# Row norms of a two-block transformer: squares as the moving operand on four column strips instead of as the stationary one

## The reference, cut to what matters

```python
def _rms_norm(x, g):
    xf = x.astype(jnp.float32)
    y = xf * lax.rsqrt(jnp.mean(xf * xf, axis=-1, keepdims=True) + EPS)
    return (y * g.astype(jnp.float32)).astype(x.dtype)
...
        h = _modulate(x, g_pre_mix[l], sx1, cx1)
        x = x + gx1 * _rms_norm(_token_mixer(h, kv_ctx, rope, lp, lam, lam_init), g_post_mix[l])
        hm = _modulate(x, g_pre_mlp[l], sx2, cx2)
        x = x + gx2 * _rms_norm(_sq_relu_mlp(hm, w_ff1[l], w_ff2[l]), g_post_mlp[l])
```

## Time and profile before

| | us |
|---|---|
| median of three runs | 3958.98 |
| lowest and highest run | 3958.79, 3963.68 |
| span of the profiled execution | 3959.9 |
| TensorE busy | 3646.2 (92%) |
| VectorE busy | 1911.9 (48%) |
| ScalarE busy | 1398.4 (35%) |
| GpSimd busy | 131.7 (3%) |

### The profile page before, as it was taken

How to read it: one execution, slowest core, us unless ns; L and a number is a source line. 1 busy time by engine, 2 the same in 40 slices (tenths; PEclk the granted TensorE clock), 3 DMA queues, 4 the chain that set the end, 5 groups by cost and what they waited for, 6 DMA issues and landing times. The chain is left out here.

```text
span 3959.9 us, 47862 instructions
## 1 busy us (share of the span) xinstructions
PE 3646.2 (92%) x18756; PEld 2836.1 (72%) x18756; DVE 1911.9 (48%) x2912; ACT 1398.4 (35%) x2388; POOL 131.7 (3%) x90
## 2 busy tenths in 40 slices
PE   6989898979999999998897999989998999989999
PEld 2878897855677778884773567778887776677767
DVE  0756565655544354441475654434443346433553
ACT  2454433224443322222423444332222435334342
POOL 0000000010000010001001000010001000000000
PEclk9999898999999989997998999989998999989999
DMA  8425453320112323326331112223332221222212
GB/s 312 149 91 155 123 165 129 100 70 28 47 60 69 107 64 93 94 91 266 123 92 36 43 49 64 85 71 95 96 96 87 67 65 51 70 89 66 60 45 94
DMA packets 97407, 371.75 MB, mean 94 GB/s; under 512 B 11184, under 2 KB 11440, under 8 KB 95280
## 3 DMA queue, kind: packets, MB, share of 16 engines
q1 hardware_dynamic: 97200, 368.82, 29.2%
HBM read 357.25 MB, written 11.53 MB: 93 GB/s over the span
## 5 line engine op out<-in xcount | busy, mean ns | idle before, releaser
L368 DVE TENSOR_TENSOR w_lo<-w_raw,w_hi 128x1024 fp32r<-128x1024 f32 x527 | 644.9, 1224 | 776.7 <-ACT w_hi L358 776.4
L382 PE MATMUL banks<-h_hi,w_hi 128*128 128x512 f32 (+2 forms) x2040 | 790.3, 387 | 28.2 <-DVE h_lo L1005 9.8
L384 PE MATMUL banks<-h_hi,w_lo 128*128 128x512 f32 (+2 forms) x2040 | 749.5, 367 | 0.0
L383 PE MATMUL banks<-h_lo,w_hi 128*128 128x512 f32 (+2 forms) x2040 | 749.3, 367 | 0.0
L358 ACT ACTIVATE w_hi<-w_raw 128x1024 fp32r<-128x1024 f32 x545 | 573.0, 1053 | 363.6 <-DMA w_raw<-in_stream 361.6
L382 PEld LDWEIGHTS banks<-h_hi,w_hi 128*128 128x128 f32 (+1 forms) x2040 | 391.1, 192 | 118.6 <-issue 35.5
L384 PEld LDWEIGHTS banks<-h_hi,w_lo 128*128 128x128 f32 (+1 forms) x2040 | 390.1, 191 | 66.4
L383 PEld LDWEIGHTS banks<-h_lo,w_hi 128*128 128x128 f32 (+1 forms) x2040 | 391.9, 192 | 56.6 <-issue 3.8
L382 PE MATMUL banks<-merged_hi,w_hi 128*128 128x512 f32 (+1 forms) x960 | 350.0, 365 | 28.1 <-PEq L2320 10.7
L384 PE MATMUL banks<-merged_hi,w_lo 128*128 128x512 f32 (+1 forms) x960 | 346.4, 361 | 0.0
L383 PE MATMUL banks<-merged_lo,w_hi 128*128 128x512 f32 (+1 forms) x960 | 345.6, 360 | 0.0
(11 more groups left out here) (322 smaller groups left out, 4988.6 us busy)
## 6 DMA issues: line engine op xcount, KB each, us to landing
w_raw<-in_stream SPq DMA_DIRECT2D x593, 512.0 KB, 3.6
w_whole<-in_stream SPq DMA_DIRECT2D x48, 512.0 KB, 8.9
x_kept<-x SPq DMA_DIRECT2D x4, 2048.0 KB, 7.2
x<-x_kept SPq DMA_DIRECT2D x4, 2048.0 KB, 8.1
dft_table<-in_dft SPq DMA_DIRECT2D x2, 2048.0 KB, 8.1
x<-in_x SPq DMA_DIRECT2D x1, 2048.0 KB, 11.2
out_x<-x SPq DMA_DIRECT2D x8, 256.0 KB, 4.4
late_consts<-in_consts SPq DMA_DIRECT2D x1, 1152.0 KB, 5.5
```

The source lines that it names most:

```text
L368: (by or self.nc.vector).tensor_tensor(self.lo[:, c], self.raw[:, c], self.hi[:, c].bitcast(F32), ALU.subtract)\
L382: self.nc.tensor.matmul(out, w_hi, x_hi, start=start, stop=False)
L383: self.nc.tensor.matmul(out, w_hi, x_lo, start=False, stop=False)
L384: mm = self.nc.tensor.matmul(out, w_lo, x_hi, start=False, stop=stop)
```

## The change

The sum of a norm over features is made the other way round. sum does nothing until four tiles are squared, and then issues four matmuls, one for each tile: the stationary operand is a 128x32 block of ones, the moving operand the whole tile of squares (512 or 256 columns), and matmul j writes 32 PSUM partitions from 32 j. The second four accumulate onto the first. A new step gather (VectorE) copies the 128 x NT result to sq[:, 0], and a new step fold (TensorE) adds the four lanes by NT/128 matmuls with the copy as the stationary operand and one column of the constant fold as the moving one; it leaves the totals with tokens on the partitions, where root reads them. average is gone. square of tile 4 to 7 now waits for the first group of four, where it waited for one tile. A bank is used for the lanes (7, or 6 where the norm's neighbour uses 7). The root of following and of the second hybrid layer's norm is taken in the stage that computes the sums.

```diff
     def square(self, act, k, src):
-        if k >= 4:
-            act.wait_ge(self.summed.sem, self.summed.at(k - 3))
+        if k >= self.LANES:
+            act.wait_ge(self.summed.sem, self.summed.at(k // self.LANES))
...
     def sum(self, pe, k):
+        if k % self.LANES < self.LANES - 1:
+            return
         pe.wait_ge(self.squared.sem, self.squared.at(k + 1))
+        for j in range(self.LANES):
+            rows = slice(self.LANE * j, self.LANE * (j + 1))
+            mm = self.K.nc.tensor.matmul(self.lane_sums[rows], self.K.const("ones")[:, 0:self.LANE], self.sq[:, j],
+                                         start=k < self.LANES, stop=k == self.n - 1, tile_position=(0, self.LANE * j))
+        mm.then_inc(self.summed.sem, 1)
+
+    def gather(self, dve):
+        dve.wait_ge(self.summed.sem, self.summed.at(self.groups))
+        self.K.nc.vector.tensor_copy(self.sq[:, 0], self.lane_sums).then_inc(self.gathered.sem, 1)
+
+    def fold(self, pe):
+        pe.wait_ge(self.gathered.sem, self.gathered.at(1))
         for i in range(self.nt):
-            at = k * self.nt + i
-            mm = self.K.nc.tensor.matmul(self.sums[:, at:at + 1], self.sq[:, k % 4, i * P:(i + 1) * P],
-                                         self.K.const("ones")[:, 0:1], start=True, stop=True)
-        mm.then_inc(self.summed.sem, 1)
-
-    def average(self, dve):
-        dve.wait_ge(self.summed.sem, self.summed.at(self.n))
-        self.K.nc.vector.reduce_sum(self.mean[:], self.sums.rearrange("p (k i) -> p i k", i=self.nt), AX_X)\
-            .then_inc(self.averaged.sem, 1)
+            mm = self.K.nc.tensor.matmul(self.totals[:, i:i + 1], self.sq[:, 0, i * P:(i + 1) * P],
+                                         self.K.const("fold")[:, 0:1], start=True, stop=True)
+        mm.then_inc(self.folded.sem, 1)
...
     def act(self, act, chunks):
...
-        self.norm.root(act)
-        if not self.squares:
+            self.norm.root(act)
+        else:
...
             post_mix.sum(pe, KD - 1)
+            post_mix.fold(pe)
             post_mix.turn(pe)
             for f in range(KD):
                 pre_mlp.sum(pe, f)
+            pre_mlp.fold(pe)
             lead.pe(pe)
...
                 following.sum(pe, KD - 1)
+                following.fold(pe)
...
+            if following is not None:
+                following.root(act)
```

More of the change, by code:

```diff
@@ L955, in pe @@
                 self.norm.sum(pe, k)
+            self.norm.fold(pe)
         self.norm.turn(pe)
@@ L1034, in rest_stage @@
         table = K.sb(scope, "table_load", [1])
[L1035 to L1037 removed]
+        post_mix = RowNorm(K, "post_mix", KD, NT, 7, 4)
+        pre_mlp = RowNorm(K, "pre_mlp", KD, NT, 6, 5)
+        post_mlp = RowNorm(K, "post_mlp", KD, NT, 7, 4)
         for norm in (post_mix, pre_mlp, post_mlp, following):
@@ L1087, in _ @@
             post_mlp.sum(pe, KD - 1)
+            post_mlp.fold(pe)
             post_mlp.turn(pe)
@@ L1106, in _ @@
                 pre_mlp.square(act, f, x[:, f, 0:NT])
+            pre_mlp.root(act)
             lead.act(act, ())
@@ L3447, in build @@
             kv_c.done = kv_x.done = True
-            before, after = after, RowNorm(K, "following", KD, SEQ, 96, 5)
+            before, after = after, RowNorm(K, "following", KD, SEQ, 6, 5)
             x = block_one_stream(K, x, vec, lam[:, l], mod[:, 0], mods[:, 0], SEQ, kv_x, [kv_x, kv_c], A["rope"],
@@ L3457, in build @@
         for l in range(2):
-            before, after = after, RowNorm(K, "pre_mix", KD, SEQ, 96, 5) if l == 0 else None
+            before, after = after, RowNorm(K, "pre_mix", KD, SEQ, 6, 5) if l == 0 else None
             h = (K.take("h_hi", [KD, SEQ], F32R), K.take("h_lo", [KD, SEQ], F32R))
```

48 lines of the change are left out of this document (24 added, 24 removed).

## The result

| | before | with the change |
|---|---|---|
| median, us | 3961.33 (four runs) | 3931.47 (four runs) |
| lowest and highest run | 3958.79, 3968.55 | 3929.97, 3934.28 |
| span of the profiled execution | 3959.9 | 3930.8 |
| TensorE busy | 3646.2 | 3565.6 |

The ratio is 0.9927, 95% interval 0.9913 to 0.9941: faster, by 23 to 34 us. The forecast was 3936 us (3926 to 3949) and a span shorter by 22.7 us; the profiled span is 29.1 us shorter. So the result lies inside the range and at its better side, and what has to be found is whether the terms are right and where 6 us more came from.

What follows compares the result with a forecast made beforehand. TensorE, busy 92% of the span, was taken as the bound. Terms -24.7 + 8.8 - 1.0 - 1.5 + 0.4 - 4.7 gave -22.7 us, so 3936 us; range 3926 to 3949 for 8 in 10.

Steps and rivals of the forecast that it cites:

- What bounds: Whole kernel: TensorE, busy 92% of the span, bounds it; time taken from TensorE inside a GEMM is time gained.
- rival D: Inside GEMMs: nothing given back, since weight DMA or splits are due at the same pace; +2.0 us, 3961; chance 0.08.
- The group: Four strip matmuls of a norm: 1.05 us at the upper clock level, 1.9 at the lower; 0.65 over 256 columns.
- the first term: Inside GEMMs: one group replaces the sums between tiles in post_mix, post_mlp, hybrid and context norms; -24.7 us together.
- Rival A: All norms: a group costs nearer 1.65 us than 1.05; +16 us, 3952; chance 0.13.
- Rival C: All norms: strips do not overlap, a group takes 3.6 us, +46 us net, 4005; chance 0.04.
- Ends of a GEMM: Last square to root behind a GEMM: 3.1 us instead of 1.45 for x, context +1.0 twice; +8.8 us together.
- rival B's other branch: Behind GEMMs: longer chain drops fold and turn to the lower clock; up to +1 us at four places, 3940; no separate chance.
- pre_mlp, pre_mix, following, hybrid end: Norms outside GEMMs and the hybrid norm's end: pre_mlp -1.0 us, pre_mix -4.7, following -1.5, hybrid end +0.4.
- The wait of square 4: ScalarE's fifth square waits for the first group: costed at nothing; 3 us once in the hybrid stage without queued blocks.
- The step of a tile without a sum back at 5.58: Sign to look for inside the GEMM of x: output tiles without a sum take 5.58 us; 6.4 would refute.

Runs made afterwards that it cites:

- GEMM only: Changed kernel with the old one-column sums put back in pre_mix, pre_mlp and following, groups only in norms behind a GEMM: 3946.5 us, ratio 0.9964.
- packed: Kernel before, all old sums kept, each norm taking 64 bytes less so that GEMM operands stand where the change has them: 3953.5 us, ratio 0.9979.
- edges only: Changed kernel with old one-column sums put back in post_mix, post_mlp and the second hybrid layer's norm: 3941.3 us, ratio 0.9945.
- the change twice: Two profiles of the changed kernel: the first, and one of an unaltered repeat, which measured 3933.6 us, ratio 0.9931.
- padded: Changed kernel with 64 unused bytes a partition for each norm, as the vector of means took before: 3940.9 us, ratio 0.9950.
- placed: Changed kernel with rest_stage's moving GEMM operands put 64 bytes past a multiple of 256 from the high weights: 3925.3 us, ratio 0.9908.
- The first profile: First profiled execution of the changed kernel, span 3930.8 us; the second is that of its unaltered repeat, 3933.6 us, ratio 0.9931.
- full width: Changed kernel with a 128x128 block of ones for each matmul of a group, so the four run in series: 3991.1 us, ratio 1.0065.

## Why the prediction was right

*What bounds.* Right for the five GEMMs over 512 tokens, not for the context's post_mlp. There TensorE's time was time gained: at the addresses of before (GEMM only), 2.4 to 2.6 us at each of the four norms of the first block, ends included, where the terms say 2.6, and 3.2 in the hybrid layer for 3.0. So rival D is out there. In the context's post_mlp it holds: the ring of splits, addition and square takes 2.99 us a tile, and once TensorE is faster than that, the ring ends last. From the first matmul to the root it took 29.4 to 31.0 us in the three profiles with the sums of before (before, packed, edges only) and 30.1 to 30.7 in five with groups (the change twice, GEMM only, padded, placed): no gain that can be told, where 1.05 was forecast. The prediction carried over the reading of the context's post_mix without this GEMM's own rows. The sum of GEMM only, -15.2 for -15.5, hides this.

*The group.* The 1.05 us was read off well where the group stands alone (1.06 behind post_mix, 1.94 for 1.9 at the lower level). Inside the GEMM it inserts 1.19 (512 columns), 0.77 (256, 3.60 - 2.83, for 0.65) and 1.23 (hybrid). With these the first term is -23.7 instead (4 x (5.34 - 1.19), 4.45 - 1.23 and twice 2.70 - 0.77) of -24.7: a size slightly off, and what the context's post_mlp has in it did not reach the time. Rival A (1.65) is out. Rival C is out too: a group in series costs 3.44 us (it said 3.6), and the kernel with it is 26 us slower than before (it said 46).

*Ends of a GEMM.* The root of x stands 3.10 behind the square at post_mix and 3.02 at post_mlp, forecast 3.1; the context's root comes 0.97 later than before, forecast 1.0. What the sum left out is rival B's other branch: in some executions the clock falls before the fold. The first profile has this at post_mlp (3.70), the second at post_mix (3.81), both in the first layer. The turn stood at the lower level behind post_mix before the change too (2.03 and 2.07).

*pre_mlp, pre_mix, following, hybrid end.* pre_mlp -0.78 and -0.80 (forecast -0.75), context +0.57 (+0.5). The root of pre_mix of x came 11.14 us after the first square (11.2), the context's came 0.8 and 1.1 us earlier in the first layer and 0.2 and 0.9 in the second (-0.6 each). The copy took 0.69 us, or 0.43 at most over 256 tokens, at all fifteen norms, so GpSimd's splits did not hold it. In the hybrid stage the inversion came 3.65 us after the end of the last square, 3.38 before: +0.3 (+0.4). For the norm following, second layer, from post_mlp's root to the inversion -1.2 (-0.75).

*The wait of square 4* was costed at nothing, and it cost nothing: in the hybrid stage ScalarE waited 13.01 us and VectorE's addition of tile 5 slipped behind a split, yet two tiles with the group between them took 17.87 us, two steps of 8.32 and 1.23.

```profile
3448.77 0.69 DVE L3386 TENSOR_TENSOR x<-x,banks 128x512 f32<-128x512 f32 x1 [2.34 <-PE banks L384]
3460.94 0.68 DVE L3386 TENSOR_TENSOR x<-x,banks 128x512 f32<-128x512 f32 x1
3466.64 0.69 DVE L3386 TENSOR_TENSOR x<-x,banks 128x512 f32<-128x512 f32 x1 [1.01 <-PE banks L384]
```

*What wasn't in the sum.* "The step of a tile without a sum back at 5.58" was wrong: it is 5.49, 5.55 or 5.60. The prediction treated the GEMMs' own rate as fixed, and the change moved their operands by 64 bytes. With the placement of before the change is worth 20.8 us in the span, 1.9 short of the forecast 22.7; the other 5 to 8 us are placement, as far as packed tells. So the forecast of 3936 came 4.5 us above the measured time, with the norms' part slightly overrated and the placement's missed. The norms' part alone, about 3940 by the padded kernel, is inside the range too; that the placement went the right way and not further is luck, since the prediction had no term for it.

*What stays open.* The long stretches move by up to 8 us between profiles, 4 between two of the same kernel. The surplus of edges only (12 us) has the size of its shorter steps, but how much of them reaches the time is open: packed has the same ones and gained 5 to 12 us by its interval. Why 64 bytes matter isn't known, nor what sets the step of the projections of h where the addresses are the same. The root of following was not put back into the next stage, since the totals would have had to stay in a PSUM bank that later stages write.

## What to carry to other kernels

Before a small gain or loss is put down to an edit, compare the step of work that the edit doesn't touch: when it has moved, the edit has moved buffers, and a kernel with the old addresses separates the two. Matmuls with few useful output rows can be put on column strips with different moving operands: four took 1.05 us here where one of full width takes 0.86. A gain read in one GEMM holds for another only if the same wait ends last there; the context's second product, 2.99 us a tile with and without the sums, shows it. And ahead of speeding up a chain, look at what its consumer waits for besides: here the turn got faster and GpSimd's weight splits kept the residual where it was.

## What was unexpected of the hardware

- Where a GEMM's moving operands stand in SBUF changes 24 matmuls of 512 columns from 5.49 to 5.60 us, by 2%, at the same clock; 64 bytes are enough, and moving all of SBUF by 64 bytes changes nothing in the MLPs. The Trainium skill, SBUF — State Buffer, section "Who interferes with whom", says that only the port pair that VectorE and GpSimd share causes contention and TensorE never waits on anyone. The runs show a price that depends on the placement; whether another engine has a part in it they don't show.
- One GEMM with the same buffers at the same addresses runs at 5.60 us a tile in one kernel and at 5.49 in another (projections of h, changed and full width).
- Whether the clock falls behind a GEMM that ends in a chain of short waits differs between executions of one kernel (turn 1.16 or 2.08 us).
- A reciprocal of 128x512 on VectorE takes 3.36 us, one of 128x4 0.18.
